# A hybrid decoder layer: h2 of the sparse block in PSUM, every second split on GpSimd, a quarter of the one-hot work on ScalarE

## The chip, the cores and the metric

The kernel runs on 1 core of a Trainium2 chip. The metric is the time of the device in microseconds (us), from the runs of the whole program.

## The reference

One layer over 512 tokens of width 1024, all float32: a mixer (mLSTM heads and latent attention), its output projection, and PEER, a retrieval of single-neuron experts. The change touches PEER alone:

```python
def block(xb):                       # 128 tokens of h = rms_norm(x)
    qry = (xb @ w_q).reshape(TB, 8, 256)
    s1 = einsum('thd,nd->thn', qry[..., :128], keys_1)   # 128 keys each
    s2 = einsum('thd,nd->thn', qry[..., 128:], keys_2)
    v1, i1 = top_k(s1, 16);  v2, i2 = top_k(s2, 16)
    sc, ci = top_k(all sums v1 + v2, 16)
    idx = i1[ci // 16] * 128 + i2[ci % 16]               # one of 16384 experts
    gate = softmax(sc)
    act = gelu(einsum('thed,td->the', u_table[idx], xb)) # exact gelu
    return einsum('the,thed->td', gate * act, v_table[idx])
```

## The kernel before

**The sparse block and the dense ones.** The 512 tokens are four blocks of 128. For the first block ("sparse"), the 128 (head, rank) slots are gathered: GpSimd fetches, for each slot, the 128 rows of `u` (`gather_u`, an indirect DMA of 512 KB into one of 8, later 4, buffers `u_rows`), and VectorE multiplies them with `h2_nat[:, 0, :]` and sums (`dot`); the same later with `v`. For the other three blocks (384 tokens, "dense") the products with all 16384 experts are made: 128 "first products", one for each block of 128 experts, then gates, then the second products.

**A first product** (`first_product`) is 24 matmuls of 128 x 384 in three parts of 8: u_hi x h2_hi, u_hi x h2_lo, u_lo x h2_hi. SP loads `u_raw` (ring of 4, `load_u(n + 4)` as soon as u_lo of block n is there), ScalarE rounds it (`round_u`: u_hi), and a split gives u_lo = u_raw - u_hi (`split_u`), which PE needs at the third part. The result goes to PSUM bank n % 4 (z); ScalarE's `gelu` writes it to `act_out`, SP saves it to a scratch tensor. Before, GpSimd splits blocks 0 to 11, and VectorE all others.

**The stages.** Pre: products 0 to 71. VectorE meanwhile chooses the experts of each token block: `choose(0)` in one go, after which the gathers can start, then `choose(1)` to `choose(3)` in pieces. A generator (`rest`) deals out pieces and dots, and the loop puts them between splits by planned sizes in ns: `SLOT_SIZE` 2800 per product, with the sizes `CHOOSE_SIZES` of the pieces and `DOT_SIZE` 1170 of a dot. 66 dots are made in pre. Main: products 72 to 119, in trips of 8. Per product two batches of 4 tokens get gate matrices on PE (`gate_matrices`): a matmul per token of `oh2` (one-hot of the second key) and `gate_rows` (one-hot of the first key times the gate). VectorE makes both (`one_hots`): one comparison of 128 x 512 for `oh2` and four of 128 x 128 for `gate_rows`. ScalarE copies the matrices out (`take_gates`). One dot per product, two in the eighth. Post: products 120 to 127, 8 dots, and the start of the second products, which fill the time from 1030 us to the end.

**What sets the order.** Each engine runs its own queue in the order of the program, and semaphores join them. ScalarE per product in pre: `round_u(n + 3)` (waits for product n - 1), `gelu(n)`; in main: `take_gates(2j)`, `round_u(n + 4)`, `gelu(n)`, `take_gates(2j + 1)`. GpSimd: its 12 splits, then all gathers of `u`, each waiting for the dot that frees its buffer (`U_BEFORE`, `dot_done`). VectorE per product: `split_u(n + 2)`, then pieces, dots or one-hots. PE waits for `uhi_ready`, for `act_ready` (the z bank is free) and, ahead of the third part, for u_lo (`wait_ulo`).

Of the kernel before, what the change touches and what calls it, by code (L numbers as in the profile page):

```python
# [15 lines left out]
P = 128  # L16
# [70 lines left out]
POOL_SPLITS = 12  # L87
# [7 lines left out]
DOTS_PRE = 66  # L95
DOTS_MAIN = [1, 1, 1, 1, 1, 1, 1, 2]
DOTS_POST = [2] * 4
assert DOTS_PRE + MAIN_TRIPS * sum(DOTS_MAIN) + sum(DOTS_POST) == SLOTS


DOT_SIZE, SLOT_SIZE = 1170, 2800
# [67 lines left out]
def build(nc, a):  # L169
    ctx = ExitStack()  # L170
    with ctx:
# [110 lines left out]

        idx0 = at("idx0", 20, [P, SLOTS], I32)
# [19 lines left out]


# [70 lines left out]
        oh_ready = sem("oh_ready")  # L375
        gate_done = sem("gate_done")
# [17 lines left out]
        dot_done = sem("dot_done")  # L394
        z0_ready = sem("z0_ready")
# [25 lines left out]
        def wait_ulo(eng, n, pool=False):  # L421

            if pool or isinstance(n, int) and n < POOL_SPLITS:
                eng.wait_ge(ulo_pool, n + 1)
            else:
                eng.wait_ge(ulo_dve, n + (1 - POOL_SPLITS))

# [9 lines left out]
        def _(sp):  # L437
# [60 lines left out]
            def pre(i, pool=False):  # L498
                for j in range(PRE_BODY):
                    n = i * PRE_BODY + j  # L500
                    wait_ulo(sp, n, pool)
# [4 lines left out]
            for i in range(POOL_SPLITS // PRE_BODY):  # L506
                pre(i, True)
            with sp.Fori(POOL_SPLITS // PRE_BODY, PRE_TRIPS) as i:
                pre(i)
# [7 lines left out]
            def main(i):  # L517
                for j in range(MAIN_BODY):
                    n = i * MAIN_BODY + (PRE + j)
                    wait_ulo(sp, n)  # L520
# [25 lines left out]
            def post_load_u(n):  # L546

                wait_ulo(sp, n)
# [64 lines left out]
        def _(pool):  # L613
# [59 lines left out]
            for n in range(POOL_SPLITS):  # L673
                split_u(n)
            pool.wait_ge(idx_ready, 1)
            for s in range(SLOTS):
                gather_u(s)

# [18 lines left out]
        def _(act):  # L697
# [229 lines left out]

            def gelu(n, j, first=False):
# [4 lines left out]
                nc.scalar.activation(act_out[:, j % RING, :], ps[:, j % RING, 0:ND], ACT.Gelu).then_inc(act_ready, 1)  # L933
# [82 lines left out]
        def _(dve):  # L1016
# [400 lines left out]
            def dot():  # L1417

                n = dots[0]
                dots[0] += 1  # L1420
                dve.wait_ge(ug_in[U_SLOT[n]], U_NTH[n] * 16 + 16)
                rows = u_rows[U_SLOT[n]]
                nc.vector.tensor_tensor_reduce(rows[:], rows[:], h2_nat[:, 0, :], 1.0, 0.0, ALU.mult, ALU.add,  # L1423
# [16 lines left out]
            def rest():  # L1440

                for t in range(1, TB):
                    made = choose(t)
                    for size in CHOOSE_SIZES:
                        if next(made, 0) is None:
                            yield size
                        if size > 1500 and dots[0] < DOTS_PRE:
                            dot()
                            yield DOT_SIZE
                while dots[0] < DOTS_PRE:  # L1450
                    dot()
                    yield DOT_SIZE

            work, done = rest(), 0
            for n in range(POOL_SPLITS - 2, PRE):
                split_u(n + 2)
                while done < (n - POOL_SPLITS + 3) * SLOT_SIZE:
                    done += next(work, SLOT_SIZE)
# [7 lines left out]
            for _ in work:  # L1466
                pass
            settle()

            def one_hots(n):  # L1470
                slot = n % OH_RING
                if n >= OH_RING:
# [3 lines left out]
                nc.vector.tensor_tensor(oh2[:, slot, :, :], bc(iota, 1, BATCH), bc(tab[:, 2, t0:t0 + BATCH], 2, NK),  # L1476
                                        ALU.is_equal).then_inc(oh_ready, 1)
# [482 lines left out]
```

## Time and profile before

| | |
|---|---|
| median of 3 runs | 1565.91 us (1565.29 to 1567.02) |
| the profiled execution | 1564.76 us, span of its instructions 1563.0 us |
| granted TensorE clock, mean | 0.989 |

The top of the page:

```profile
span 1563.0 us, 22972 instructions
## 1 busy us (share of the span) xinstructions
PE 1515.3 (97%) x8069; PEld 1353.2 (87%) x8069; DVE 1223.1 (78%) x2336; ACT 561.5 (36%) x816; POOL 547.2 (35%) x297
## 2 busy tenths in 40 slices
PE   6999989999989999999999999979999999999999
PEld 6879658788989999999999999968888888888887
DVE  4537473288989999989999999648878788787886
ACT  4363442222423333334444444333232332322321
POOL 2213241232643222752333323314434434344341
PEclk9999979999999999999999999999999999999999
DMA  5400202221467877997798898999999999999993
GB/s 198 142 28 1 108 1 67 87 75 68 162 226 266 276 260 258 367 413 289 296 324 311 284 332 309 356 327 373 354 350 355 352 356 354 351 359 349 354 355 125
```

The first part gives each engine's busy time, its share of the span and its instructions. The second cuts the span in 40 slices of 39 us: each digit is the busy share in tenths (9 is 90% and more), and PEclk is the granted clock in tenths of full speed. The front (mixer, projections, queries) takes slices 0 to 9, the first products run from slice 10 to 26, the second products from there to the end. VectorE's row is near 9 in slices 11 to 24, GpSimd's is low.

### The profile page before, as it was taken

The page shows a single profiled execution, that of the slowest core. Times are in us where ns is not written, and L with a number is a line of the kernel's source. Part 1 is how long each engine was busy: PE and PEld are TensorE (multiplying, and loading weights), DVE is VectorE, ACT ScalarE, POOL GpSimd, SP SyncE. Part 2 cuts the span into 40 slices and gives each one's busy share as a digit, 9 for nine tenths or more (in the row PEclk, how much of TensorE's full clock was granted, in tenths as well). Part 3 has the DMA queues.
Part 4 walks back from the last instruction along what each step waited for, and adds up shares of the span by engine and source line. Part 5 has one row for each costly group of instructions (what it writes and reads, how often), then busy time and mean ns, then how long its engine had stood idle before and what let it go on. Part 6 is the DMA issues. An engine that isn't in the chain of part 4 may idle for free.

```text
span 1563.0 us, 22972 instructions
## 1 busy us (share of the span) xinstructions
PE 1515.3 (97%) x8069; PEld 1353.2 (87%) x8069; DVE 1223.1 (78%) x2336; ACT 561.5 (36%) x816; POOL 547.2 (35%) x297
## 2 busy tenths in 40 slices
PE   6999989999989999999999999979999999999999
PEld 6879658788989999999999999968888888888887
DVE  4537473288989999989999999648878788787886
ACT  4363442222423333334444444333232332322321
POOL 2213241232643222752333323314434434344341
PEclk9999979999999999999999999999999999999999
DMA  5400202221467877997798898999999999999993
GB/s 198 142 28 1 108 1 67 87 75 68 162 226 266 276 260 258 367 413 289 296 324 311 284 332 309 356 327 373 354 350 355 352 356 354 351 359 349 354 355 125
DMA packets 181667, 399.37 MB, mean 256 GB/s; under 512 B 12260, under 2 KB 111844, under 8 KB 180072
## 3 DMA queue, kind: packets, MB, share of 16 engines
q1 hardware_dynamic: 144744, 264.41, 48.3%
q0 software_dynamic: 36864, 134.23, 23.3%
q8 instruction: 30, 0.49, 0.1%
q14 instruction: 29, 0.24, 0.0%
HBM read 346.16 MB, written 52.43 MB: 255 GB/s over the span
## 4 chain that ended last, share of the span: by engine, by line
PE 83%; DVE 8%; POOL 3%; DMA 3%; issue 1%; ACT 1%; SPq 0%; DVEq 0%; ACTq 0%
PE banks L1820 25%; PE banks L1613 15%; PE banks L1884 11%; PE banks L1886 11%; PE banks L1885 11%; PE banks L1855 5%; POOL u_rows L669 3%; DMA u_rows<-in_u,idx 1%; DMA v_raw<-in_v 1%; PE banks L1801 1%; PE banks L1664 1%; DVE wo_lo L1241 1%; PE banks L1723 1%; DVE picked L1385 1%; PE banks L1748 1%
## 5 line engine op out<-in xcount | busy, mean ns | idle before, releaser
L669 POOL DMA_INDIRECT u_rows<-in_u,idx x128 | 202.9, 1585 | 362.8 <-DVE z L1423 336.7
L691 POOL DMA_INDIRECT v_rows<-in_v,idx x128 | 205.5, 1606 | 333.4 <-DVE x_res L1550 294.8
L1884 PE MATMUL banks<-v_hi,w_hi 128*128 128x512 f32 x768 | 299.6, 390 | 7.4 <-DVE v_lo L1497 7.4
L1886 PE MATMUL banks<-v_hi,w_lo 128*128 128x512 f32 x768 | 299.3, 390 | 0.0
L1885 PE MATMUL banks<-v_lo,w_hi 128*128 128x512 f32 x768 | 299.3, 390 | 0.0
L1497 DVE TENSOR_TENSOR v_lo<-v_raw,v_hi 128x1024 fp32r<-128x1024 f32 x128 | 153.6, 1221 | 120.4 <-ACT v_hi L982 120.4
L982 ACT ACTIVATE v_hi<-v_raw 128x1024 fp32r<-128x1024 f32 x128 | 125.8, 1049 | 339.0 <-PE banks L1886 320.2
L1820 PE MATMUL banks<-h_lo,u_hi 128*128 128x384 f32 x1024 | 209.9, 338 | 0.0
L1820 PE MATMUL banks<-h_hi,u_lo 128*128 128x384 f32 x1024 | 199.2, 335 | 9.5 <-DVE u_lo L1412 9.5
L1820 PE MATMUL banks<-h_hi,u_hi 128*128 128x384 f32 x1024 | 203.6, 340 | 0.3 <-ACT u_hi L909 0.3
L1820 PEld LDWEIGHTS banks<-h_hi,u_lo 128*128 128x128 f32 x1024 | 179.4, 188 | 11.1 <-DVE u_lo L1412 11.1
L1820 PEld LDWEIGHTS banks<-h_hi,u_hi 128*128 128x128 f32 x1024 | 177.7, 189 | 0.6 <-ACT u_hi L909 0.6
L1820 PEld LDWEIGHTS banks<-h_lo,u_hi 128*128 128x128 f32 x1024 | 177.3, 188 | 0.0
L1884 PEld LDWEIGHTS banks<-v_hi,w_hi 128*128 128x128 f32 x768 | 144.5, 188 | 37.7 <-issue 7.8
L1886 PEld LDWEIGHTS banks<-v_hi,w_lo 128*128 128x128 f32 x768 | 144.4, 188 | 30.3
L1885 PEld LDWEIGHTS banks<-v_lo,w_hi 128*128 128x128 f32 x768 | 144.6, 188 | 29.9
L1550 DVE SCALAR_TENSOR_TENSOR x_res<-v_rows,w,x_res 128x1024 f32<-128x1024 f32 x128 | 163.8, 1280 | 0.9
L1423 DVE CUSTOM_DVE_ANT_0 u_rows<-u_rows,h_nat 128x1024 f32<-128x1024 f32 x128 | 154.4, 1221 | 8.9 <-DMA u_rows<-in_u,idx 6.7
L903 ACT ACTIVATE u_hi<-u_raw 128x1024 fp32r<-128x1024 f32 x122 | 128.8, 1057 | 84.3 <-PE banks L1820 69.5
L1412 DVE TENSOR_TENSOR u_lo<-u_raw,u_hi 128x1024 fp32r<-128x1024 f32 x116 | 141.2, 1220 | 12.4 <-ACT u_hi L909 8.6
L933 ACT ACTIVATE act_out<-banks 128x384 f32<-128x384 f32 x128 | 62.1, 485 | 194.1 <-PE banks L1820 180.7
L1480 DVE TENSOR_SCALAR gate_rows<-consts,tab 128x128 f32<-128x128 f32 x384 | 107.0, 347 | 0.0
(256 smaller groups left out, 1926.2 us busy)
## 6 DMA issues: line engine op xcount, KB each, us to landing
u_raw<-in_uT SPq DMA_DIRECT2D x128, 512.0 KB
v_raw<-in_v SPq DMA_DIRECT2D x128, 512.0 KB, 5.9
act_scratch<-act_out SPq DMA_DIRECT2D x128, 192.0 KB
act_in<-act_scratch SPq DMA_DIRECT2D x32, 768.0 KB, 8.4
gates<-gate_scratch SPq DMA_DIRECT2D x32, 768.0 KB, 12.4
gate_scratch<-stage SPq DMA_DIRECT2D x11, 2048.0 KB, 8.1
wi_raw<-in_w_in SPq DMA_DIRECT2D x8, 1024.0 KB, 8.7
wq_raw<-in_w_q SPq DMA_DIRECT2D x8, 1024.0 KB, 5.6
```

The lines of the kernel that those rows point to most:

```text
L669: nc.gpsimd.indirect_dma_start(u_rows[U_SLOT[s]][:], None, a["u"], bass.IndirectOffsetOnAxis(ap=idx0[:, s:s + 1], axis=0)).then_inc(ug_in[ ...
L691: nc.gpsimd.indirect_dma_start(v_rows[s % V_ROWS][:], None, v_flat, bass.IndirectOffsetOnAxis(ap=idx0[:, s:s + 1], axis=0)).then_inc(vg_in ...
L903: nc.scalar.activation(u_hi[:, j % 4, :, :], u_raw[:, j % 4, :, :], ACT.Copy).then_inc(uhi_ready, 1)
L1412: nc.vector.tensor_tensor(u_lo[:, slot, :, :], u_raw[:, n % 4, :, :], u_hi[:, slot, :, :].bitcast(F32), ALU.subtract).then_inc(ulo_dve, 1)
L1423: nc.vector.tensor_tensor_reduce(rows[:], rows[:], h2_nat[:, 0, :], 1.0, 0.0, ALU.mult, ALU.add, z0[:, n:n + 1]).then_inc(dot_done, 1)
L1497: nc.vector.tensor_tensor(v_lo[q][:, j, :], v_raw[:, j, :], v_hi[q][:, j, :].bitcast(F32), ALU.subtract).then_inc(vlo_ready, 1)
L1550: nc.vector.scalar_tensor_tensor(out=x_res[:, 0, :], in0=v_rows[n % V_ROWS][:], scalar=w0[:, n:n + 1], in1=x_res[:, 0, :], op0=ALU.mult, o ...
L1613: last = mm(o, lhs(x, k), rhs(y, k), start=n == k == 0, stop=n == 2 and k == KD - 1)
L1820: last = mm(o, u[:, q, k, :], h2[:, k, T0:], start=m == 0, stop=m == PER_BLOCK - 1)
L1884: mm(y, w, v_hi[q][:, j, ds], start=first and j == 0, stop=False)
L1885: mm(y, w, v_lo[q][:, j, ds], start=False, stop=False)
L1886: end = mm(y, w_lo[q][:, j, t * P:(t + 1) * P], v_hi[q][:, j, ds], start=False, stop=last and j == GROUP - 1)
```

## The change

1. h2 of the sparse block, 1024 columns, is copied by ScalarE from `h2_nat[:, 0, :]` to PSUM banks 2 and 3 (`h2_first`), behind `round_u(2)` and ahead of the first gelu. The dots read it there. The first products have two z banks (0, 1) instead of four.
2. From block 16 on, GpSimd makes every second split (16, 18, ... 118: 52 splits), VectorE the others. Where VectorE would have made it, it writes one element per partition (`memset`) and thereby opens GpSimd's split (`share_open`); two dots follow the memset. GpSimd's queue mixes these splits with the gathers of `u`.
3. The dots are placed by a table `DOTS_AT`: two at each such place, one more at every second odd n from 55 to 69 and at n = 77, 83, ... 119, two at each of 120 to 123. The first dot comes at n = 14. The choose pieces are dealt by their own sizes, 2150 ns per product.
4. In main, `oh2` of every odd batch is made by ScalarE (`one_hot`): four squares of (t - iota), 128 columns each, then Relu of 1 - square over 512 columns. It stands behind `take_gates(2j)`, for batch 2j + 3. VectorE makes `oh2` of the even batches and all `gate_rows`.

The diff, cut to its core:

```diff
-POOL_SPLITS = 12
+POOL_FIRST, SHARE_FROM = 12, 16
+Z_BANKS = 2
-DOTS_PRE = 66
-DOTS_MAIN = [1, 1, 1, 1, 1, 1, 1, 2]
-DOTS_POST = [2] * 4
+SHARED = list(range(SHARE_FROM, POST, 2))
+DOTS_AT = [2 if n + 2 in SHARED else 0 for n in range(POST)] + [2] * 4 + [0] * 4
+for _n in [*range(PRE - 17, PRE, 2)][:8] + [*range(PRE + 5, POST, 6)]:
+    DOTS_AT[_n] += 1
-DOT_SIZE, SLOT_SIZE = 1170, 2800
+PIECE_SIZE = 2150
...
+        h2_first = ps[:, 2:4, :].rearrange("p b d -> p (b d)")
...
 # GpSimd
-            for s in range(SLOTS):
+            s = 0
+            for n in range(len(DOTS_AT)):
+                while s < SLOTS and (U_BEFORE[s] is None or U_BEFORE[s] < sum(DOTS_AT[:n])):
+                    gather_u(s)
+                    s += 1
+                if n + 2 in SHARED:
+                    pool.wait_ge(share_open, SHARED.index(n + 2) + 1)
+                    split_u(n + 2)
...
 # ScalarE
+            for j in (2, 3):
+                emptied(act, JOBS[(len(JOBS) - 1) // 8 * 8 + j][0])
+            nc.scalar.activation(h2_first, h2_nat[:, 0, :], ACT.Copy).then_inc(h2_placed, 1)
...
-                nc.scalar.activation(act_out[:, j % RING, :], ps[:, j % RING, 0:ND], ACT.Gelu).then_inc(act_ready, 1)
+                nc.scalar.activation(act_out[:, j % RING, :], ps[:, j % Z_BANKS, 0:ND], ACT.Gelu).then_inc(act_ready, 1)
...
+            def one_hot(i, b):
+                slot, m = b % OH_RING, i * (MAIN_BATCHES // 2) + (b // 2)
+                for w in range(BATCH):
+                    at_t = tab[:, 2, bass.ds(i * (MAIN_BATCHES * BATCH) + (b * BATCH + w), 1)]
+                    nc.scalar.activation(oh2[:, slot, w, :], iota, ACT.Square, bias=at_t, scale=-1.0
+                                         ).then_inc(oh_square, 1)
+                act.wait_ge(oh_square, m * BATCH + BATCH)
+                nc.scalar.activation(oh2[:, slot, :, :], oh2[:, slot, :, :], ACT.Relu, bias=1.0, scale=-1.0
+                                     ).then_inc(oh_scalar, 1)
+            act.wait_ge(tab_ready, 1)
+            one_hot(0, 1)
...
                     take_gates(i, 2 * j, first)
+                    if not (last and j == MAIN_BODY - 1):
+                        one_hot(i, 2 * j + 3)
...
 # VectorE
-                nc.vector.tensor_tensor_reduce(rows[:], rows[:], h2_nat[:, 0, :], 1.0, 0.0, ALU.mult, ALU.add,
+                nc.vector.tensor_tensor_reduce(rows[:], rows[:], h2_first, 1.0, 0.0, ALU.mult, ALU.add,
...
+            def splits_and_dots(n):
+                if n + 2 in SHARED:
+                    nc.vector.memset(opened[:, SHARED.index(n + 2):SHARED.index(n + 2) + 1], 0.0).then_inc(share_open, 1)
+                else:
+                    split_u(n + 2)
+                for _ in range(DOTS_AT[n]):
                     dot()
...
+            for n in range(POOL_FIRST - 2, PRE):
+                splits_and_dots(n)
+                while done < (n - POOL_FIRST + 3) * PIECE_SIZE:
+                    done += next(sizes)
+                    next(work, None)
...
+                if n % 2 == 0:
+                    nc.vector.tensor_tensor(oh2[:, slot, :, :], bc(iota, 1, BATCH),
+                                            bc(tab[:, 2, t0:t0 + BATCH], 2, NK), ALU.is_equal).then_inc(oh_ready, 1)
...
-                    split_u(PRE + i * MAIN_BODY + j + 2)
+                    splits_and_dots(PRE + i * MAIN_BODY + j)
...
 # PE
-                    pe.wait_ge(act_ready, n - (RING - 1))
-                o, q = ps[:, j % RING, 0:ND], j % ring
+                    pe.wait_ge(act_ready, n - (Z_BANKS - 1))
+                o, q = ps[:, j % Z_BANKS, 0:ND], j % ring
```

## Rows read from the trace of the kernel before

**Rows 1.** the page, busy time, share of the span and instructions of an engine

```profile
PE 1515.3 (97%) x8069; PEld 1353.2 (87%) x8069; DVE 1223.1 (78%) x2336; ACT 561.5 (36%) x816; POOL 547.2 (35%) x297
```

**Rows 2.** stretches: us, busy time of each engine with records, TensorE's granted clock, DMA

```profile
464.00:640.00 176.00, 176.00 (x1017) 176.00 (x1016) 172.78 (x336) 62.63 (x86) 53.67 (x32) 1.00 0.82 271
...
710.00:980.00 270.00, 270.00 (x1818) 270.00 (x1817) 264.75 (x615) 114.57 (x183) 84.39 (x51) 1.00 0.85 307
...
456.00:460.00 4.00, 3.57 (x13) 3.58 (x14) 3.11 (x28) 0.49 (x1) 2.86 (x4) 0.66 1.00 378
```

**Rows 3.** waits of PE in 400 to 470 and 600 to 710 us: total, times, longest

```profile
PE banks L1820 <- DVE u_lo L1412: 5.6, 3, 3.5
...
PE banks L1855 <- DVE gate_rows L1480: 0.5, 1, 0.5
```

**Rows 4.** timeline around the first dot: start, us, engine, line, operation [idle before]

```profile
448.50 1.66 PE L1820 MATMUL banks<-h_hi,u_lo 128*128 128x384 f32 x8 [1.24 <-DVE u_lo L1412]
...
450.00 1.55 PE L1820 MATMUL banks<-h_hi,u_hi 128*128 128x384 f32 x8
...
454.00 1.23 DVE L1423 CUSTOM_DVE_ANT_0 u_rows<-u_rows,h_nat 128x1024 f32<-128x1024 f32 x1 [3.33 <-DMA u_rows<-in_u,idx]
...
455.15 1.22 DVE L1412 TENSOR_TENSOR u_lo<-u_raw,u_hi 128x1024 fp32r<-128x1024 f32 x1
...
456.43 2.22 PE L1820 MATMUL banks<-h_hi,u_lo 128*128 128x384 f32 x8 [3.48 <-DVE u_lo L1412]
456.55 0.35 SPq L482 DMA_DIRECT2D u_raw<-in_uT  x1
...
458.44 2.60 PE L1820 MATMUL banks<-h_hi,u_hi 128*128 128x384 f32 x8
...
460.88 1.57 PE L1820 MATMUL banks<-h_lo,u_hi 128*128 128x384 f32 x8
...
462.05 1.22 DVE L1412 TENSOR_TENSOR u_lo<-u_raw,u_hi 128x1024 fp32r<-128x1024 f32 x1
...
463.31 1.68 PE L1820 MATMUL banks<-h_hi,u_lo 128*128 128x384 f32 x8 [0.86 <-DVE u_lo L1412]
...
463.64 1.06 ACT L903 ACTIVATE u_hi<-u_raw 128x1024 fp32r<-128x1024 f32 x1 [4.46 <-DMA u_raw<-in_uT]
```

**Rows 5.** durations of single lines (min/median/max), then groups with mean ns

```profile
L1423 DVE CUSTOM_DVE_ANT_0 u_rows<-u_rows,h_nat x128: 1208/1220/1232, 454.0 to 1008.9; 128x1024 f32<-128x1024 f32 x128
...
L662 POOL TENSOR_TENSOR u_lo<-u_raw,u_hi x12: 2387/2391/5643, 380.8 to 429.6; 128x1024 fp32r<-128x1024 f32 x12
...
L783 ACT ACTIVATE junk<-kv_nat x16: 309/310/312, 104.0 to 110.5; 128x128 f32<-128x128 f32 x16
...
L933 ACT ACT_TABLE_LOAD  x2: 1283/1283/1283, 395.3 to 664.0; - x2
...
L1290 DVE TENSOR_TENSOR h_lo<-banks,h_hi 128x512 fp32r<-128x512 f32 x8 | 5.5, 688 | 0.7
...
L669 POOL DMA_INDIRECT u_rows<-in_u,idx x128: 937/1681/3949, 447.6 to 999.4; - x128
...
L943 ACT ACTIVATE sc_v<-sc_v 128x512 f32<-128x512 f32 x1 | 0.6, 633 | 0.0
```

**Rows 6.** timeline, GpSimd and VectorE at the same time in two places

```profile
425.25 9.98 POOL L662 TENSOR_TENSOR u_lo<-u_raw,u_hi 128x1024 fp32r<-128x1024 f32 x2 [1.78 <-ACT u_hi L903]
...
427.39 5.57 DVE L1385 TENSOR_TENSOR picked<-picked,pay 128x3200 f32<-128x3200 f32 x1
...
477.62 3.48 DVE L1385 TENSOR_TENSOR picked<-picked,pay 128x3200 f32<-128x3200 f32 x1
477.97 3.95 POOL L669 DMA_INDIRECT u_rows<-in_u,idx  x1 [6.47 <-DVE z L1423]
```

**Rows 7.** timeline as the first products start

```profile
397.35 0.50 DVE L1327 MAX8 best_v<-banks 128x8 f32<-128x128 f32 x2
...
402.92 0.49 ACT L933 ACTIVATE act_out<-banks 128x384 f32<-128x384 f32 x1 [2.72 <-PE banks L1820]
```

More of the change, by code:

```diff
@@ L504, in pre @@
                         save_act(n - 2, j + 2)
-            for i in range(POOL_SPLITS // PRE_BODY):
-                pre(i, True)
-            with sp.Fori(POOL_SPLITS // PRE_BODY, PRE_TRIPS) as i:
+            for i in range(SHARE_FROM // PRE_BODY):
+                pre(i)
+            with sp.Fori(SHARE_FROM // PRE_BODY, PRE_TRIPS) as i:
                 pre(i)
@@ L1439, in _ @@
                 pass
[L1440 to L1450, printed above, removed]
-                    dot()
[L1452 to L1458, printed above, removed]
+            def splits_and_dots(n):
+                if n + 2 in SHARED:
+                    nc.vector.memset(opened[:, SHARED.index(n + 2):SHARED.index(n + 2) + 1], 0.0).then_inc(share_open, 1)
+                else:
+                    split_u(n + 2)
+                for _ in range(DOTS_AT[n]):
+                    dot()
+            work, done = itertools.chain(*(choose(t) for t in range(1, TB))), 0
+            sizes = itertools.cycle(CHOOSE_SIZES)
+            for n in range(POOL_FIRST - 2, PRE):
[3 more added lines that the diff above has]
+                    next(work, None)
                 if n == NORM_AT:
@@ L1465, in _ @@
                                                    ps[:, 4 + t, 0:3 * P].rearrange("p (w t) -> p w t", w=3)))
-            for _ in work:
-                pass
+            assert next(work, 0) == 0
             settle()
+            dve.sem_inc(tab_ready, 1)
             def one_hots(n):
@@ L1490, in _ @@
                             one_hots(i * MAIN_BATCHES + 2 * j + 2 + n)
-                    for _ in range(DOTS_MAIN[j]):
-                        dot()
             def split_v(g, q, j):
@@ L1516, in post_dots @@
             def post_dots(n):
-                for _ in range(DOTS_POST[n - POST]):
+                for _ in range(DOTS_AT[n]):
                     dot()
@@ L1827, in _ @@
             assert RING <= INDEX[("s12", PH - 1, 0)] % 8
[L1828 to L1834 removed]
+            for n in range(SHARE_FROM):
+                if n < Z_BANKS:
+                    emptied(pe, JOBS[(len(JOBS) - 1) // 8 * 8 + n][0])
+                first_product(n, n, 0, n, 1, first=n < Z_BANKS)
+            with pe.Fori(SHARE_FROM // PRE_BODY, TRI_TRIP) as i:
                 for j in range(PRE_BODY):
[L1836 removed]
+                    first_product(i * PRE_BODY + j, j, i, j, PRE_BODY)
             for n in range(TRI_TRIP * PRE_BODY, PRE):
@@ L1860, in main @@
                     between = [((b + 1) * PER_BATCH - 1 - j * PER_BLOCK,
-                                lambda b=b: gate_matrices(i * MAIN_BATCHES + b, b, first and b < 4))
+                                lambda b=b: gate_matrices(i, b, first and b < 4))
                                for b in BATCHES_IN[j]]
-                    first_product(i * MAIN_BODY + (PRE + j), j, between=between)
+                    first_product(i * MAIN_BODY + (PRE + j), j, i, PRE + j, MAIN_BODY, between=between)
             main(0, True)
```

64 lines of the change are left out of this document (39 added, 25 removed).

## The prediction

> **What bounds the kernel now.** I read the busy shares first: PE works in 97% of the span [rows 1]. Then the stretches: in 464 to 640 us PE issues 1017 matmuls in 176 us, with no gap. A first product is 24 matmuls, so one takes 176 x 24 / 1017 = 4.15 us (I use 4.16, as the timeline spaces them). In 710 to 980 us it issues 1818 in 270 us; a product with its two batches of gate matrices is 24 + 16 records, so 5.94 us, again without a gap [rows 2]. A faster VectorE or ScalarE is worth nothing there. What can be won is only where PE waits, so I read the waits of PE next: between 400 and 470 us it waits three times for u_lo, 5.6 us in all, and once 0.5 us for gate_rows at 705.7 us [rows 3]. The waits after 1000 us (behind the first products) are for work which this change leaves as it is.
>
> The timeline tells why the 5.6 us arise [rows 4]. The first wait, 1.24 us, ends with the split of block 12, which VectorE can only do behind choose(0); that order is unchanged. Product 13 starts at 450.00. The second, 3.48 us, ends with the split of block 13: VectorE had idled 3.33 us ahead of it for the rows of its very first dot, so without that dot it would have been ready at 454.00 - 3.33 = 450.67. The third is 0.86 us. After the second wait the granted clock is 0.66 of 2.4 GHz on average over 456 to 460 us [rows 2], between the levels 1.2 and 2.4 GHz: eight matmuls take 458.44 - 456.43 = 2.01 and then 460.88 - 458.44 = 2.44 us in place of 4.16 / 3 = 1.39, so the wait costs 0.62 + 1.05 = 1.67 us more [rows 4].
>
> **The change part by part.** *First dots.* They come at n = 14 and not behind the first piece of choose(1). VectorE then does split 13 from 450.67 to 451.8, and PE needs it at 450.0 + 2.77 = 452.8: no wait. Next come the pieces planned at 1.0 and 3.1 us; on the timeline they lie between the end of split 13 (456.29, its start 455.15 + 1.14) and 462.05, so 5.76 us, of which the trace calls 1.5 to 1.9 us idle for no visible reason. With 5.76 us split 14 ends at 458.7, and PE needs it at 450.0 + 4.16 + 2.77 = 456.9: a wait of 1.9 us. With 3.9 us (no idle time) it ends at 456.8: no wait. I take 1.0 us, between the two, because the trace doesn't show whether that idle time comes back, and no loss of clock, since rows of the stretch behind the 1.24 us wait show none. Split 15 follows directly (459.9 at the latest, needed at 461.1 or later). Gain: 3.48 + 0.86 + 1.67 - 1.0 = 5.0 us.
>
> *Splits moved to GpSimd.* 52 of VectorE's 116 splits go, 29 of them ahead of main. GpSimd takes 2.39 us for one when nothing holds it [rows 5]. What it collides with is visible once: the split of GpSimd that stands at 425.25 and a VectorE instruction with both inputs in SBUF, 5.57 us long instead of 3.48, thus held 2.1 us; GpSimd's two splits take 9.98 us in place of 4.8 [rows 6]. So the place counts. The memset lets the split begin as two dots begin: 2 x 1.15 = 2.3 us (a dot lasts 1.22, and the next starts 1.15 behind its start) [rows 4, 5], in which VectorE reads only one operand in SBUF. The split sticks out by 2.39 + 0.1 - 2.3 = 0.2 us, if GpSimd is free. It may not be: a gather is held by the same kind of VectorE instruction, 3.95 us at 477.97 beside picked at 477.62 [rows 6], against 0.94 for a free one [rows 5]; two gathers stand between two splits, and where the second is held the split starts late by up to 1 to 2 us.
>
> The Trainium skill, page "SBUF — State Buffer", section "Who interferes with whom", has a DVE instruction with two SBUF inputs contend with a GpSimd instruction that reads SBUF, not with descriptor generation. The 3.95 us row speaks against its second half; by the page the split would never be late, the collisions would be 0.2 us a pair, the sum the same and rival (b) half as likely.
>
> A pair of products in pre now costs VectorE: pieces 2 x 2.15 = 4.30 by the plan (the plan's 3.35 us piece measures 3.40, the small ones measure less), one split 1.14, a memset 0.08 (no row: between 0.07 and 0.2, like its smallest instructions; I take the accumulator read's 0.08), two dots 2.30, together 7.8 us, against 2 x 4.16 = 8.32. So 0.5 us of headroom for collisions of 0.2 to 1.1 us per pair. Carrying these terms forward from 447 us, step by step, with the ring and the gathers, collisions add up to some 2 to 6 us over the 20 pairs of the choose phase, about 0.3 a pair, and VectorE stays ahead of PE's need with less than 0.3 us of new waits. That is inside the 1.0 us above. From n = 54 on there are no pieces, and VectorE needs 5 to 6 us of 8.32. In main a pair costs 0.08 + 1.14 + 2.33 x 1.15 + 16 x 0.28 + 2 x 0.62 = 9.6 of 11.9 us. The 0.5 us wait at 705.7 goes, since VectorE then has its one-hots ready: +0.5 us.
>
> *h2 in PSUM.* With operands in SBUF, 1024 columns take 1220 ns [rows 5] and 3200 take 3480 [rows 6], so a column 1.04 and 512 columns 1220 - 532 = 688 ns. An instruction that reads 512 columns of a bank takes 688 [rows 5]: no cost for the 128 dots. No row shows a dot with such an operand; its own spread, 1.208 to 1.232 us, bounds it at 0.02 us either way, and I take 0. The copy itself, 1024 columns, about 1.05 us on ScalarE, must wait till VectorE has emptied bank 2, about 397.3 (the next head's first maximum starts at 397.35). Then copy to 398.4, u_hi(3) to 399.4, the table load of 1.28, and the first gelu ends at about 401.2. Behind it in ScalarE's queue are u_hi(3), whose split and product come at 409 or later, and gelu 0, for which product 2 now waits (two z banks): it starts at 402.5 (the gelu of product 1 follows at 402.92) [rows 7]. Cover 1.3 us; were it gone, each us late would be a us of PE. Cost 0.
>
> *Two z banks.* Product n waits for gelu n - 2, which ends some 0.6 us into product n - 1, 3.5 us early. SP's and ScalarE's queues now matter more: gelu stands behind a round that waits for a load.
>
> *One-hots on ScalarE.* Nearest row: a Square of 128 columns out of SBUF, 0.31 us [rows 5]; without the accumulator, with a bias operand, overlapped, I bound one between 0.2 and 0.4 and take 0.3. Relu over 512 columns: 0.63 by the 512-column Exp [rows 5]. 4 x 0.3 + 0.1 wait + 0.63 = 1.95 us per product (1.5 to 2.4). ScalarE is busy 114.57 us in 45.4 products = 2.52 us each [rows 2]. Sum 4.5 of 5.94 us, so it is hidden; what is queued behind (round, gelu, take_gates) has 4 us to spare. From 3.4 us on it would bound.
>
> **Sum.** 5.0 + 0.5 = 5.5 us. The profiled execution takes 1564.76 us (span 1563.0 and 1.8 around it): 1559.3 for it; against the median 1565.91: **1560.4 us**. A measurement here tells differences above 0.2% (3.1 us).
>
> **Rivals.** (a) *Swallowed.* A late load stalls PE through the two z banks. The load issued at 456.55 lets u_hi start only at 463.64, 7.1 us later, while eight gathers fill the DMA [rows 4]. Issued at 456.9 after the change, it gives u_hi(18) at 465.1 and gelu(15) at 465.5, and product 17 starts at 466.7. It decides at a latency of 8.3 us, and beyond that costs us for us; two or three such stalls, or a first dot at n = 14 that waits, and a longer idle time of VectorE, take 2.5 to 5.5 us: 1563 to 1566, no change. Against it: the plan spreads the dots. 22%.
>
> (b) *Slower: the port.* GpSimd is regularly late or the dot still holds the port in spite of PSUM (the change then doesn't do what it says). Each pair of the choose phase then costs up to 2.39 us more: 7.8 + 2.4 = 10.2 against 8.32, 1.9 x 20 = 38 us, less the 5.5 us gained: 1598; with 1.3 us a pair 0.8 x 20 = 16, less 5.5: 1576. It decides at 0.5 us a pair, from where the gain shrinks, and is slower from about 0.9. For it: the 3.95 us gathers. Against: the durations of free gathers, 0.94. 11%.
>
> (c) *Slower: tables.* If Square or Relu isn't in Gelu's table set, each product in main has two loads of 1.283 us [rows 5]: 4.5 + 2.6 = 7.1 against 5.94, 1.15 x 48 = 55 us: 1615. Copy runs between gelus without a load, Square between Sqrt, but neither Square nor Relu beside Gelu is in the trace. The Trainium skill, page "ScalarE: Activation LUTs", section "Table sets: the hidden batching unit", counts relu and copy in every set and doesn't name square there; by its 2.66 us for a switch the price would be double. 5%.
>
> **Chances.** Forecast 62% (1557 to 1562.7), (a) 22%, (b) 11%, (c) 5%. Range 1557 to 1568: below, the gain without any new wait is 6.5 us (1559.4), and 2.4 us for products behind 1000 us that start at another phase; above, it takes in (a) and the mildest form of (b). Faster 0.62, same 0.22, slower 0.16.
>
> **What would show it.** PE's waits for u_lo between 450 and 470 us fall from 4.3 to about 1 us and the clock stays 1.00; product 72 starts about 5 us earlier; PE has no idle time from there to 980 us; GpSimd's splits read 2.39 us and the instruction behind the dots is no longer than before; L1385 of 5.6 us would show (b); PE waits for act_out would show (a); ACT_TABLE_LOAD rows in main (c). Square over 0.4 us, a dot over 1.3 us, or waits of ScalarE's gelu behind loads that reach PE make the prediction wrong.

## The result, and the profile after

The changed kernel takes 1557.03 us, the median of 5 runs (1555.51 to 1558.27), where the kernel before took 1565.62 us beside it: ratio 0.9944, 95% interval 0.9930 to 0.9958, so 8.6 us less. On another chip the same kernel gave 1557.43 us and 0.9945 (0.9932 to 0.9957). The forecast was 1560.4 us; the time lies at the lower edge of the range. The direction and most of the mechanisms were right; the gain is 3.1 us larger than the sum, because terms of the sum were wrong. Two single executions, 3907 us of the run with one early dot and 3072 us of the run with two z banks, are left out of every comparison.

First the busy shares of the changed kernel's page, the line that answers to [rows 1].

```profile
PE 1512.1 (97%) x8069; PEld 1351.5 (87%) x8069; DVE 1146.0 (74%) x2288; ACT 643.0 (41%) x1057; POOL 630.3 (41%) x349
```

VectorE has 77 us less to do, ScalarE and GpSimd some 82 us more each. TensorE's busy time differs by 3 us. Next the stretches, with the columns of [rows 2], and TensorE's waits from 390 to 1050 us (total, times, longest).

```profile
464.00:640.00 176.00, 176.00 (x1018) 176.00 (x1017) 164.75 (x338) 63.90 (x87) 126.34 (x71) 1.00 0.92 326
...
710.00:980.00 270.00, 270.00 (x1818) 270.00 (x1817) 213.06 (x549) 189.49 (x407) 106.53 (x74) 1.00 0.85 306
```

```profile
PE banks L1938 <- DVE v_lo L1547: 6.8, 1, 6.8
PE banks L1870 <- DVE u_lo L1464: 3.6, 2, 2.3
```

The long stretches are paced by TensorE as before, with the same number of matmuls; the time of VectorE that came free in them (51.7 us in 710 to 980) buys nothing there. The 3.6 us of waits for u_lo are the 1.24 us of block 12, which stayed, and 2.32 us at 1009.17 us. The 3.48 and 0.86 us of [rows 4] and the 0.5 us for gate_rows of [rows 3] are gone.

The gain by place is read from the starts of the same matmuls in both timelines. Of the kernel before, the first row is that at 448.50 us in [rows 4]; then product 72 (the first with gate matrices), product 120 (the first behind them), the first matmul of the second products, and the one that waits for v_lo:

```profile
702.97 1.55 PE L1820 MATMUL banks<-h_hi,u_hi 128*128 128x384 f32 x8
...
989.14 1.63 PE L1820 MATMUL banks<-h_hi,u_hi 128*128 128x384 f32 x8
...
1027.61 0.39 PE L1884 MATMUL banks<-v_hi,w_hi 128*128 128x512 f32 x1
...
1051.55 0.76 PE L1884 MATMUL banks<-v_hi,w_hi 128*128 128x512 f32 x1 [7.42 <-DVE v_lo L1497]
```

The same five of the changed kernel:

```profile
449.65 1.68 PE L1870 MATMUL banks<-h_hi,u_lo 128*128 128x384 f32 x8 [1.24 <-DVE u_lo L1464]
...
697.67 1.55 PE L1870 MATMUL banks<-h_hi,u_hi 128*128 128x384 f32 x8
...
983.02 1.63 PE L1870 MATMUL banks<-h_hi,u_hi 128*128 128x384 f32 x8
...
1020.58 0.39 PE L1938 MATMUL banks<-v_hi,w_hi 128*128 128x512 f32 x1
...
1043.93 0.77 PE L1938 MATMUL banks<-v_hi,w_hi 128*128 128x512 f32 x1 [6.83 <-DVE v_lo L1547]
```

| stretch | before | after | difference |
|---|---|---|---|
| block 12's u_lo to product 72 | 254.47 | 248.02 | -6.45 |
| product 72 to 120 | 286.17 | 285.35 | -0.82 |
| product 120 to the second products | 38.47 | 37.56 | -0.91 |
| to the wait for v_lo | 23.94 | 23.35 | -0.59 |
| from there to the end of the span | 511.45 | 511.27 | -0.18 |

That is 8.95 us. The two profiled spans differ by only 7.8 us (1563.0 and 1555.2), because the changed kernel's profiled execution reached the first row 1.15 us later (449.65 against 448.50). In the other traced executions of both kernels and their variants the stretch ahead of it moves by as much and more, so this is no effect of the change; the medians, 8.6 us apart, agree with the table.

### The profile page after: what moved, and what is told of

It is laid out like the page before. It is cut to its first block, busy times and chain, and to the rows that moved or that the text cites. A ratio compares the mean times of both kernels' runs of the same rounds, so it can differ in the third digit from the quotient of the medians.

```text
span 1555.2 us, 23439 instructions
## 1 busy us (share of the span) xinstructions
PE 1512.1 (97%) x8069; PEld 1351.5 (87%) x8069; DVE 1146.0 (74%) x2288; ACT 643.0 (41%) x1057; POOL 630.3 (41%) x349
## 4 chain that ended last, share of the span: by engine, by line
PE 89%; DVE 7%; DMA 1%; ACT 1%; issue 1%; SPq 0%; DVEq 0%; ACTq 0%
PE banks L1870 30%; PE banks L1663 15%; PE banks L1938 11%; PE banks L1940 11%; PE banks L1939 11%; PE banks L1909 5%; DMA v_raw<-in_v 1%; PE banks L1851 1%; PE banks L1714 1%; DVE wo_lo L1293 1%; PE banks L1773 1%; DVE picked L1437 1%; PE banks L1798 0%; PE banks L1792 0%; DVE e_f L1440 0%
## 5 line engine op out<-in xcount | busy, mean ns | idle before, releaser
L683 POOL TENSOR_TENSOR u_lo<-u_raw,u_hi 128x1024 fp32r<-128x1024 f32 x64 | 158.5, 2478 | 195.6 <-DVE opened L1497 151.2
L690 POOL DMA_INDIRECT u_rows<-in_u,idx x128 | 161.6, 1263 | 103.1 <-DVE z L1477 65.1
L1477 DVE CUSTOM_DVE_ANT_0 u_rows<-u_rows,banks 128x1024 f32<-128x1024 f32 x128 | 150.7, 1214 | 0.0
```

What stands on the lines that cost most here:

```text
L683: nc.gpsimd.tensor_tensor(u_lo[:, n % 4, :, :], u_raw[:, n % 4, :, :], u_hi[:, n % 4, :, :].bitcast(F32), ALU.subtract).then_inc(ulo_pool, 1)
L690: nc.gpsimd.indirect_dma_start(u_rows[U_SLOT[s]][:], None, a["u"], bass.IndirectOffsetOnAxis(ap=idx0[:, s:s + 1], axis=0)).then_inc(ug_in[ ...
L1477: nc.vector.tensor_tensor_reduce(rows[:], rows[:], h2_first, 1.0, 0.0, ALU.mult, ALU.add, z0[:, n:n + 1]).then_inc(dot_done, 1)
```

## The experiments

**The first dots' order alone.** The kernel before, with its first dot moved behind the fourth large piece.

```diff
+            dealt = [0]
...
-                        if size > 1500 and dots[0] < DOTS_PRE:
+                        dealt[0] += 1
+                        if size > 1500 and dealt[0] > 4 and dots[0] < DOTS_PRE:
```

> The kernel before with one edit: no dot behind the first four pieces of choose(1), so the first dot comes about 7 us later. All splits stay on VectorE, h2 in SBUF, four z banks. Theory A (the gain in pre is the order of the first dots alone): PE's 3.48 and 0.86 us waits near 456 and 463 us and the low clock behind them go, nothing comes in their place: 6.5 us less than before, about 1559.1. Theory B (VectorE was full, and the idle time that is taken away comes back as a later wait, so the gain needs the splits on GpSimd): less than 3 us gained, above 1562.6, and PE waits for u_lo somewhere between 470 and 700 us.

1563.98 us, ratio 0.9991 (0.9982 to 1.0): next to nothing. Its timeline, TensorE's rows and then VectorE's:

```profile
466.73 1.67 PE L1823 MATMUL banks<-h_hi,u_lo 128*128 128x384 f32 x8 [1.11 <-DVE u_lo L1412]
...
698.06 1.55 PE L1823 MATMUL banks<-h_hi,u_hi 128*128 128x384 f32 x8
...
702.33 1.49 PE L1858 MATMUL banks<-gate_rows,oh 128*128 128x128 f32 x8 [2.02 <-DVE gate_rows L1483]
...
704.90 2.25 PE L1823 MATMUL banks<-h_hi,u_lo 128*128 128x384 f32 x8
```

```profile
698.28 1.22 DVE L1423 CUSTOM_DVE_ANT_0 u_rows<-u_rows,h_nat 128x1024 f32<-128x1024 f32 x1
...
701.16 1.11 DVE L1483 TENSOR_SCALAR gate_rows<-consts,tab 128x128 f32<-128x128 f32 x4
```

The 3.48 us wait is gone, a new one of 1.11 us for u_lo has come at 466.73 us, and TensorE is at product 72 at 698.06 us, 4.9 us earlier than before. (The prediction's numbers for this stretch, 1.0 us of new wait and 5.0 us gained, come out here and not in the changed kernel, but by luck: the wait is for block 16, and the prediction had it at block 14.) But VectorE ends its last dot only 3.4 us earlier (its next instruction at 699.42 instead of 702.83). So TensorE waits 2.02 us at the gates, and runs slower behind that wait (2.25 us where eight such matmuls take 1.55 by themselves): product 73 starts at 707.80 instead of 709.65. Of 4.9 us, 1.85 are left there. At the start of the second products 1.04 us are left, since the eight matmuls behind a wait of 2.33 us took 2.8 us there and 1.7 in the kernel before; at the end of the span it is 0.8 us. The theory that the order alone gives the gain fell.

**The same with four dots fewer ahead of product 72.**

```diff
-DOTS_PRE = 66
+DOTS_PRE = 62
-DOTS_POST = [2] * 4
+DOTS_POST = [3] * 4
```

> The kernel before with the first dot product dealt to the fifth large piece, as in the run with only that edit, and four dot products moved from ahead of product 72 to behind product 119 (DOTS_PRE 62, DOTS_POST three at each of four places). In the run with the late first dot alone TensorE reached product 72 at 698.06 us instead of 702.97 us, 4.9 us earlier, but VectorE's last dot only at 699.4 instead of 702.8, and a wait of 2.02 us for gate_rows with a low clock behind it gave 3.1 us back. Theory B2 (that debt of VectorE at the entry of the gated products is what returned the gain): four dots less are 4 x 1.23 = 4.9 us less work ahead of the first gate_rows, the wait of 2.02 us goes, the gain of 4.9 us stays but for 0 to 1 us: 1559.5 to 1561 us, ratio 0.9965 to 0.998, unless eight dots turned into twelve behind product 119 lengthen the waits there. Rival C (the gain is lost elsewhere, by the loads behind product 119 or by gathers that come no earlier): the wait at 702 goes but the time stays at 1563 to 1565 us.

1567.98 us, ratio 1.0013 (1.0002 to 1.0024). Both halves of the expectation are answered by its trace, whose execution took 1563.34 us, the fastest of the 11:

```profile
1005.32 2.69 PE L1823 MATMUL banks<-h_hi,u_lo 128*128 128x384 f32 x8 [3.98 <-DVE u_lo L1412]
...
1013.83 1.66 PE L1823 MATMUL banks<-h_hi,u_lo 128*128 128x384 f32 x8 [2.48 <-DVE u_lo L1412]
```

TensorE is at product 72 at 696.32 us and at product 73, without a wait at the gates, 5.86 us later (6.68 in the kernel before, 9.74 with the order alone): VectorE's debt had caused it. The four dots then cost their time behind product 119, where the waits are 3.98, 2.48, 0.46 and 1.63 us instead of 2.33, 0.29 and 1.61: 4.3 us more. The other ten executions were slower still, and no trace tells why. I had named that risk and taken it for small. Moving the dots along VectorE's queue, behind product 119, gained nothing; what did is to take work off VectorE.

**The changed kernel with one early dot.** The other way round: one dot ahead of the landing of its gather, everything else kept.

```diff
+DOTS_AT[POOL_FIRST - 2] += 1
+DOTS_AT[PRE - 17] -= 1
```

> The changed kernel with one dot product moved from the 55th product's place to the one behind the split of block 12, so that VectorE meets it before its gather has landed, as in the kernel before. There the gather landed at 454.0 us, VectorE stood 3.3 us and TensorE 3.48 us. Theory (order counts in full where VectorE has slack): TensorE waits for u_lo 13 from 453.9 us to about 458.7, some 4 to 5 us, with 1 to 2 us of low clock behind it, and nothing is won back, since TensorE bounds the stretch: 5 to 6.5 us above the changed kernel, 1562 to 1563.5 us, ratio 0.997 to 0.9985. Rival (order doesn't count, since GpSimd's splits let VectorE catch up): less than 2 us above the changed kernel, below 1559 us.

1566.36 us, ratio 1.0005 (0.9995 to 1.0014): the whole gain is gone, more than expected. VectorE's row, then TensorE's:

```profile
454.93 1.22 DVE L1479 CUSTOM_DVE_ANT_0 u_rows<-u_rows,banks 128x1024 f32<-128x1024 f32 x1 [6.21 <-DMA u_rows<-in_u,idx]
```

```profile
459.60 2.93 PE L1872 MATMUL banks<-h_hi,u_lo 128*128 128x384 f32 x8 [6.39 <-DVE u_lo L1466]
```

VectorE stands 6.21 us ahead of the dot, since the gather landed 0.9 us later than at 454.0 and the 2.3 us of pieces that were done meanwhile now come behind the dot. TensorE stands 6.39 us, and eight matmuls behind it take 2.93 instead of 1.55. Nothing is won back later. But this isn't quite the kernel before's order: its first dot came behind those 2.3 us of pieces, this one ahead of them. TensorE waits 2.9 us longer than there (6.39 against 3.48), and the three groups behind the wait lose 2.76 us to the low clock (466.52 - 459.60 - 4.16) instead of 1.67. So with the dot where the kernel before had it, this kernel would take some 4.0 us less, 1562.4 us or 0.998; that is an estimate from these rows, and no run tried it. What is shown: the order without room on VectorE gives 0.9991, both give 0.9944, and a dot that is too early costs 9 us even where there is room. That room without the order is worth nothing is not shown; by the estimate it is worth about 3 us.

**h2 in SBUF.** The changed kernel with the dots reading h2 where they did before.

```diff
-                nc.vector.tensor_tensor_reduce(rows[:], rows[:], h2_first, 1.0, 0.0, ALU.mult, ALU.add,
+                nc.vector.tensor_tensor_reduce(rows[:], rows[:], h2_nat[:, 0, :], 1.0, 0.0, ALU.mult, ALU.add,
```

> The changed kernel, but the dots read h2 from SBUF (the copy in PSUM is still made). Theory A (the shared port decides, and the PSUM operand is what lets a split run beside a dot): each opened split holds VectorE's next instruction with two SBUF inputs, about 2.4 us a pair of products, so VectorE needs 10.2 us for 8.32 in the choose phase: some 20 to 38 us slower than the changed kernel, 1577 to 1595, with dots of 1.2 to 3.6 us. Theory B (GpSimd has slack and waits till the dots are through, VectorE loses nothing): within 3 us of the changed kernel's 1557.0.

1588.87 us, ratio 1.0155 (1.0138 to 1.0171), 32 us above the changed kernel. Groups from 464 to 980 us of this kernel (busy us, mean ns of one, idle before), then TensorE's waits from 390 to 1060 us:

```profile
L1477 DVE CUSTOM_DVE_ANT_0 u_rows<-u_rows,h_nat 128x1024 f32<-128x1024 f32 x116 | 239.8, 2101 | 0.0
...
L683 POOL TENSOR_TENSOR u_lo<-u_raw,u_hi 128x1024 fp32r<-128x1024 f32 x51 | 159.2, 3121 | 133.2 <-DVE opened L1497 127.7 <-ACT u_hi L934 5.4
```

```profile
PE banks L1870 <- POOL u_lo L683: 13.5, 9, 2.6
PE banks L1870 <- DVE u_lo L1464: 12.1, 14, 2.3
```

and the same two groups of the changed kernel in that stretch:

```profile
L1477 DVE CUSTOM_DVE_ANT_0 u_rows<-u_rows,banks 128x1024 f32<-128x1024 f32 x120 | 141.3, 1214 | 0.0
...
L683 POOL TENSOR_TENSOR u_lo<-u_raw,u_hi 128x1024 fp32r<-128x1024 f32 x52 | 124.6, 2397 | 167.7 <-DVE opened L1497 151.2 <-ACT u_hi L934 16.3
```

With two operands in SBUF a dot takes 2.10 us on average in this stretch instead of 1.21, and a split of GpSimd 3.12 instead of 2.40. This is rival (b) made real: TensorE waits 23 times for u_lo, in the changed kernel twice. The operand in PSUM is what makes the sharing pay.

**Splits not opened.** GpSimd splits when the block is there, without the wait for the memset.

```diff
-                    pool.wait_ge(share_open, SHARED.index(n + 2) + 1)
```

> The changed kernel, but GpSimd's shared splits don't wait for the memset: they start as soon as u_hi is there and GpSimd's queue is at them. Theory A (the opening is needed): a split then often begins beside a two-input piece and holds the next one for up to 2.4 us; VectorE's headroom of 0.5 us a pair is overdrawn in the choose phase: 3 to 20 us slower than 1557.0, the picked instruction (3.5 us alone) often 4 to 6 us, new waits of PE for u_lo before 620 us. Theory B (headroom is enough): within 2 us of 1557.0.

1559.58 us, ratio 0.9958 (0.9942 to 0.9973). That lies between the two theories, and the interval overlaps with the changed kernel's, so what the opening is worth, about 2 us, isn't told by the times. VectorE's busy time grows by 55 us in the trace. The instruction that Theory A named, picked, isn't longer (3.48 us on average of six from 452 to 650 us, 3.86 in the changed kernel); there VectorE's own splits are, 1.73 us on average instead of 1.27. A part of this nobody had foreseen; 710 to 980 us, here and then in the changed kernel:

```profile
L1531 DVE TENSOR_SCALAR gate_rows<-consts,tab 128x128 f32<-128x128 f32 x360 | 140.9, 463 | 15.6 <-PE banks L1908 15.6
```

```profile
L1532 DVE TENSOR_SCALAR gate_rows<-consts,tab 128x128 f32<-128x128 f32 x356 | 99.0, 348 | 43.2 <-PE banks L1909 43.2
```

Instructions with a single SBUF tensor as input take 463 instead of 348 ns on average beside unopened splits. TensorE has two more short waits for u_lo, 1.6 us, and none of this reaches it in the gated products, as VectorE has 17 us to spare there even so.

**One-hots back on VectorE.** The changed kernel with all second-key one-hots on VectorE.

```diff
-                    if not (last and j == MAIN_BODY - 1):
-
-                        one_hot(i, 2 * j + 3)
...
-                if n % 2 == 0:
+                if True:
```

> The changed kernel, but VectorE makes the second-key one-hots of all batches again, none on ScalarE. Theory A (once the splits are shared, VectorE has room in main: 9.6 + 1.4 = 11.0 of 11.9 us a pair): the same time as the changed kernel, 1557.0 within 1 us, ScalarE about 110 us busy in 710 to 980 us in place of 189. Theory B (ScalarE's part is what keeps VectorE ahead): PE waits for gate_rows or u_lo in main, 2 us or more slower.

1558.11 us, ratio 0.9949 (0.9935 to 0.9962), and TensorE's waits for u_lo are those of the changed kernel. VectorE is busy 240.18 us in 710 to 980 us and still never late. Moving the one-hots gave nothing that can be measured.

**Two z banks in the kernel before.**

```diff
-                o, q = ps[:, j % RING, 0:ND], j % ring
+                o, q = ps[:, j % 2, 0:ND], j % ring
...
```

> The kernel before with z in two banks of PSUM instead of four and nothing else. Step (vi) of the prediction took this as free. Theory: within 1 us of the kernel before, no wait of TensorE for act_out. Rival: TensorE waits for act_out in the stretch of the gated products or behind product 119, over 2 us slower. It also shows whether the two banks are why the waits of 1.61 and 0.29 us at 1021.94 and 1017.26 us are gone in the changed kernel: if they stay here, it is not the banks.

1565.43 us, ratio 0.9996 (0.9987 to 1.0005): no cost, as the prediction has it under "Two z banks" (the text above calls it step (vi)). But the trace has a wait that rival (a) described, behind product 119:

```profile
1016.21 1.68 PE L1820 MATMUL banks<-h_hi,u_lo 128*128 128x384 f32 x8 [2.33 <-DVE u_lo L1412]
...
1020.18 1.74 PE L1820 MATMUL banks<-h_hi,u_hi 128*128 128x384 f32 x8 [2.28 <-ACT act_out L933]
```

It stands in place of 0.29 us for u_hi and 1.61 us for u_lo, which came of late loads too. The gelu in question stood on ScalarE behind the rounding of block 126, which waited for its load till 1018.60 us. So the banks turn one kind of wait into another; they don't explain why the changed kernel has neither.

**Three waits that were left.** First GpSimd splits block 12 too:

```diff
-POOL_FIRST, SHARE_FROM = 12, 16
+POOL_FIRST, SHARE_FROM = 13, 16
```

> The changed kernel with GpSimd splitting block 12 too (POOL_FIRST 13), ahead of the gathers. In the changed kernel TensorE waits 1.24 us at 449.65 us for u_lo 12 of VectorE, which comes behind three instructions of 3.5 us. Theory: that wait goes, and 1.2 us with it (clock of the stretch was 1.00): 1555 to 1556.5 us, ratio 0.993 to 0.994. Rival: GpSimd's split of block 12 pushes the first gathers back by its 2.4 us or more, and dots 0 and 1 at 461.5 us find their rows late, so that the time is the same or up to 2 us longer.

1554.13 us, ratio 0.9925 (0.9911 to 0.9938), about 1 us better than expected, which is inside the interval. TensorE has no wait from 440 to 1000 us in its trace, so the rival's late rows didn't come. Then two moves behind product 119:

```diff
+            post_load_u(POST + 2)
             sp.dma_start(last[:, GROUP:, :].rearrange("p n t -> p (n t)"),
...
-                post_load_u(POST + j)
...
+            split_u(POST + 5)
```

> The changed kernel with two moves behind product 119: VectorE makes the split of block 125 ahead of the second pair of splits of v, and the queue of SyncE loads block 126 ahead of the last gates' write. TensorE waits 2.32 us at 1009.17 us for u_lo 125, and the two groups of eight matmuls behind it take 2.61 and 2.02 us instead of 1.39 us. Theory: wait and low clock go, 2.3 to 4 us: 1553 to 1555 us, ratio 0.992 to 0.9935. Rival: the wait only moves to the load of the next block or to v_lo at 1043.93 us, which now takes 6.83 us, and the time stays within 1 us of the changed kernel's.

1555.66 us, ratio 0.9932 (0.9919 to 0.9946), 0.0012 below the changed kernel's and within both intervals. As the rival had it, the wait moved; it was split rather than removed:

```profile
1010.11 1.65 PE L1871 MATMUL banks<-h_hi,u_hi 128*128 128x384 f32 x8 [1.48 <-ACT act_out L969]
...
1014.33 1.68 PE L1871 MATMUL banks<-h_hi,u_lo 128*128 128x384 f32 x8 [1.18 <-DVE u_lo L1465]
```

The first is new: gelu waits till block 120's activations are saved, and that save still stood far back on SyncE's queue. So the next kernel moves this save ahead of it too, and the loads of the second group of v ahead of the last four saves:

```diff
+            save_act(POST, 0)
+            post_load_u(POST + 2)
             sp.dma_start(last[:, GROUP:, :].rearrange("p n t -> p (n t)"),
...
+            for j in range(GROUP):
+                sp.wait_ge(vlo_ready, j + 1)
+                load_v(GROUP + j, j)
             for j in range(RING):
                 save_act(POST + RING + j, j)
```

> The changed kernel with four moves: GpSimd splits block 12 too; VectorE splits block 125 ahead of the second pair of splits of v; SyncE saves block 120's activations and loads block 126 ahead of the last gates' write, which in the run of that move alone held its queue for 6.7 to 8.5 us; and SyncE loads the second group of v ahead of the last four saves of activations, instead of at 1023.6 us behind them. In the changed kernel the waits of TensorE from 440 to 1050 us are 1.24, 2.32 and 6.83 us. Theory (each wait is the end of one chain that these moves shorten): 1.2 + 1.5 to 3 + 5 to 7.5 = 8 to 11.5 us less than the changed kernel, 1545.5 to 1549 us, ratio about 0.988. Rival (the loads are bound by their bytes, the mean DMA share is 0.95 from 980 to 1050 us): the v_lo wait shrinks by no more than 2 us, since the loads only change places; 1552 to 1555 us.

> The changed kernel once more, beside the other two, so that they can be compared on one chip: 1556 to 1558 us, ratio 0.993 to 0.996.

1546.83 us, ratio 0.9876 (0.9861 to 0.9890), beside 1557.43 us of the changed kernel on the same chip: 10.6 us less, inside the 8 to 11.5 us of the theory. TensorE's waits over its whole trace hold no v_lo any more. Its queue of SyncE and the first matmul of its second products, and then the same loads in the changed kernel:

```profile
1007.95 6.10 SPq L554 DMA_DIRECT2D v_raw<-in_v  x4
```

```profile
1018.97 0.39 PE L1944 MATMUL banks<-v_hi,w_hi 128*128 128x512 f32 x1
```

```profile
1023.59 2.19 SPq L554 DMA_DIRECT2D v_raw<-in_v  x4
```

The loads are issued 15.6 us earlier, and the 6.83 us wait, for which the page named VectorE's v_lo, was a place in a queue. From the first second product to the end of the span it takes 1545.2 - 1018.97 = 526.2 us instead of 1555.2 - 1020.58 = 534.6: 8.4 us less, the wait and 1.6 us of low clock behind it (in the changed kernel the granted clock is 0.50 from 1043.9 to 1046 us and 0.78 to 1048). One u_lo wait, 2.61 us at 1011.71, is left, now for block 126: its split began at 1010.44 us, directly behind w_lo on VectorE, while its u_hi had been rounded at 1002.26. It is no load that is late there, but the split's place among the weights' work.

## Why the prediction was right or wrong

*Which step failed.* The mechanism of the gain was right, terms of the sum were not. The sum said 5.5 us, the traces 8.95. The 3.45 us between them are: 1.50 us behind product 119, which the prediction put at nothing ("for work which this change leaves as it is") without a row for it; 1.0 us for a new wait that it subtracted and that measured 0; 0.45 and 0.32 us that waits cost beyond their idle time, at the first dots and at the gates; and 0.18 us at the end. The step that failed most is the first of these, and its cause is open in part.

*The first dots.* The mechanism was right, and the order is needed: the run with one early dot, though its dot stands earlier than the old one, loses more than the whole gain. The size was off. Block 12's u_lo to product 72 gave 6.45 us, not 5.0. 1.0 of this is the new wait that I had subtracted. The changed kernel's VectorE row:

```profile
456.77 2.35 DVE L1464 TENSOR_TENSOR u_lo<-u_raw,u_hi 128x1024 fp32r<-128x1024 f32 x2
```

The pieces between split 13 and this one run from 452.87 to 456.77 and take 3.9 us, the lower of my two values (5.76 and 3.9), and the split is ready in time. The idle time of VectorE "for no visible reason" in the kernel before is in none of the twelve other traces, the run with two z banks and the old order included. As far as these show it was a mishap of one execution, and so was the wait of 0.86 us; the run with two z banks has 4.32 us as its second wait in place of 3.48 and 0.86, and takes 254.09 us for the stretch, so the total to be won was the same. The remaining 0.45 us are 6.45 - 3.48 - 0.86 = 2.11 instead of the 1.67 of low clock that I summed. They aren't low clock: by [rows 4] the first matmul behind each of the two waits starts 0.18 us after the idle time is over (452.77 + 3.48 = 456.25 against 456.43; 460.88 + 1.39 + 0.86 = 463.13 against 463.31), and the eight behind the second take 1.52 us instead of 1.39 although the granted clock is 1.00 from 463.30 to 465.00 us. A wait moves what follows by 0.2 to 0.3 us more than the idle time that the trace gives it.

*What I left out.* I treated the order as an edit that pays alone and the splits as one that needs to be free. The two are one: the order alone returns 3.1 of 4.9 us at the gates. The sum for the whole change wasn't hurt by this, as both are in it, but a reader of my text would have made only the cheap half.

*The wait at the gates.* 0.5 was forecast for it. Product 72 to 120 gave 0.82: the 0.52 us wait, 0.16 us between the end of its idle time and the first matmul, and 0.13 us in the groups behind it.

*Behind product 119.* I wrote that the waits after 1000 us are for work which this change leaves as it is, and counted 0; the range held 2.4 us for products that start at another phase. 1.50 us came. The waits of 0.29 and 1.61 us went; behind the wait of 2.32 us two groups of eight matmuls took 1.7 us more than at full clock, where before they took 0.4 us more; and the v_lo wait fell from 7.42 to 6.83 us. Block 126's load is issued at 1005.10 us before and at 997.30 us after, 15.96 and 14.28 us behind product 120's start:

```profile
995.54 8.48 SPq L570 DMA_DIRECT2D gate_scratch<-stage  x1
```

```profile
988.72 7.54 SPq L591 DMA_DIRECT2D gate_scratch<-stage  x1
```

The first fence is of the kernel before, the second of the changed one, both SyncE's queue: the issue ahead of the load is held for 8.48 and 7.54 us. It isn't the two banks and isn't the one-hots: the run with the banks alone keeps a wait of 2.28 us there, and the one with VectorE's one-hots has none. It isn't the order of the first dots either: the run with that alone has a wait of 1.27 us, and the one with an early dot has none. With h2 back in SBUF and all else kept the load is late again, 17.70 us behind product 120's start, and two short waits (0.69 and 1.20 us) are back. That leaves GpSimd's splits beside dots that read PSUM, and the dots' places in the gated products; by which way they let the queue go on earlier wasn't tried, and stays open.

*Splits on GpSimd.* Right in its steps. The timeline of the changed kernel at the first pair:

```profile
461.52 1.22 DVE L1477 CUSTOM_DVE_ANT_0 u_rows<-u_rows,banks 128x1024 f32<-128x1024 f32 x1
461.55 0.06 DVE L1497 MEMSET opened<- 128x1 f32 x1
```

```profile
461.71 2.39 POOL L683 TENSOR_TENSOR u_lo<-u_raw,u_hi 128x1024 fp32r<-128x1024 f32 x1 [0.54 <-DVE opened L1497]
...
471.79 4.02 POOL L690 DMA_INDIRECT u_rows<-in_u,idx  x1 [0.15 <-issue]
```

The memset costs 0.06 us (0.08 taken), the split begins 0.16 us behind it and takes the free 2.39. The collisions that I put at 0.3 us a pair fall on L1437, which from 452 to 650 us takes 3.86 us on average of six (3.48 before), and on VectorE's own splits, 1.27 us on average of 27 (1.22 before): 2.3 and 1.6 us, some 3.8 in all, within my 2 to 6, and no wait of TensorE came of them. A gather again took 4.02 us beside L1437, which started at 471.34 us. The Trainium skill, page "SBUF — State Buffer", section "Who interferes with whom", infers that such an instruction doesn't contend with descriptor generation: both traces speak against it (all such gathers are counted in the last section).

*h2 in PSUM.* Right: a dot takes 1214 ns instead of 1220, the copy 1.03 us (it began at 398.41 us, 1 us later than I had it, inside the cover of 1.3), and rival (b) comes with 32 us when the operand goes back, between my 1576 and 1598.

*One-hots.* Right in time and of no worth. Groups of the changed kernel:

```profile
L1002 ACT ACTIVATE oh<-consts,tab 128x128 f32<-128x128 f32 x192 | 60.9, 392 | 0.0
L1005 ACT ACTIVATE oh<-oh 128x512 f32<-128x512 f32 x48 | 30.3, 631 | 1.5
```

One Square reads 392 ns, at the edge of my bound of 0.4, but they overlap: the busy time is 60.9 / 192 = 0.32 us each. 4 x 0.32 + 0.63 = 1.9 us per product (1.95 taken). No table load stands in the gated products, so rival (c) is out. The Trainium skill, page "ScalarE: Activation LUTs", section "Table sets: the hidden batching unit", doesn't list square for Gelu's set; these 192 Squares beside Gelu needed none.

*Rival (a)*, at 22%, didn't come: the changed kernel has no wait for act_out at all, though three variants show it behind product 119: 2.28 and 0.69 us where the load of block 126 is late, and 1.48 us where the save of block 120's activations is.

## What to carry to other kernels

A wait that is removed on a full engine comes back where that engine next has to be on time: before counting such a gain, follow the engine's backlog to the next place where TensorE needs it, and price the wait and that backlog together. A wait named after an engine can be a place in a DMA queue; where the split waits for a rounding and that for a load, look at what the load's issue stood behind. Where GpSimd's splits run beside VectorE, choose what VectorE does meanwhile: here the dots shared well with one operand in PSUM (1.21 us) and badly with both in SBUF (2.10 us). And give a wait that you count more than its idle time, here 0.2 to 0.3 us, before any low clock.

## What the runs showed of the hardware that I hadn't expected

- Instructions of VectorE with one SBUF tensor and two pointers, 128 columns, took 463 instead of 348 ns on average where GpSimd's splits ran beside them at any time. By the Trainium skill, page "SBUF — State Buffer", section "Who interferes with whom", a tensor_scalar can be in a mode that takes both ports; the numbers agree.
- Indirect gathers were held beside VectorE's instructions of 3200 columns with two inputs in SBUF. From 452 to 620 us 4 gathers of the kernel before and 9 of the changed one took 3.08 to 4.04 us; each began while such an instruction ran, and ended 0.8 us behind its end. The 12 gathers that began beside L1388 or L1440, as long but with one input, took 0.93 to 0.95 us.
- The issue on SyncE's queue that came behind the first loads of gates was held for 8.48 us before and 7.54 us after, the last gates' write (7.25 to 9.26 us in eight more runs, 13.50 us in the one with twelve dots behind product 119); where a load of block 126 stood in that place it was held for 6.67 us, and where a save of activations did, for 7.53 us, while the write then took 1.50. The place on the queue is held, whatever of these three stands there.
- After a wait of TensorE of 2.32 us the groups of eight matmuls followed in 2.61 and 1.86 us (1.39 free) in the changed kernel; in the kernel before, behind 2.33 us, the first took 1.67 and the second 1.52. The same wait doesn't always cost the same clock, so a sum that carries a stall's clock over from another place is off by 1 us and more.
